# Moving the recurrent gate products of a pair of tiles behind both columns of the attention branch

## The reference, cut to what matters

```
xc = conv_b + sum_k conv_w[k] * shift(u_lru, k)                  # 4 taps
r = sigmoid(xb @ w_rg + b_rg);  i = sigmoid(xb @ w_ig + b_ig)    # 16 blocks of 64 features
log_a = -8 * r * softplus(-lru_lambda);  a = exp(log_a)
b = sqrt(-expm1(2 * log_a)) * (i * xc);  h_t = a_t * h_{t-1} + b_t
merged = g0 * (y_pool @ w_branch[0]) + g1 * (h @ w_branch[1]) + g2 * (y_sb @ w_branch[2])
```

## Time and profile before

| | |
|---|---|
| Median of 3 runs | 2202.89 us (2202.59 to 2204.14) |
| Profiled execution, its own time | 2201.45 us |
| Its span | 2199.6 us |
| Granted TensorE clock, mean | 0.997 |
| Busy: PE, PEld | 99%, 81% |
| Busy: DVE, ACT, POOL | 38%, 39%, 48% |
| Chain that ended last | PE 92%, DVE 4%, ACT 2% |

### The profile page before, as it was taken

How to read it: one execution, slowest core, us unless ns; L and a number is a source line. 1 busy time by engine, 2 the same in 40 slices (tenths; PEclk the granted TensorE clock), 3 DMA queues, 4 the chain that set the end, 5 groups by cost and what they waited for, 6 DMA issues and landing times.

```text
span 2199.6 us, 27553 instructions
## 1 busy us (share of the span) xinstructions
PE 2169.8 (99%) x10078; PEld 1788.5 (81%) x10078; DVE 844.8 (38%) x1310; ACT 855.8 (39%) x1209; POOL 1048.3 (48%) x882
## 2 busy tenths in 40 slices
PE   8999999999999999999999999999999999999998
PEld 6778777888888888888888888888887888888887
DVE  4244667632451111222376632322226555233212
ACT  4245686422242222222366533332224734333321
POOL 5431245655554444555455444445554535444553
PEclk9999999999999999999999999999999999999999
DMA  5221122322222222233221232223332212222222
GB/s 178 90 78 67 39 96 77 115 96 96 96 96 95 95 98 78 102 104 114 87 79 47 77 115 95 95 77 104 104 105 91 77 48 92 98 97 101 83 98 78
DMA packets 33848, 201.37 MB, mean 92 GB/s; under 512 B 3884, under 2 KB 6188, under 8 KB 15340
## 3 DMA queue, kind: packets, MB, share of 16 engines
q1 hardware_dynamic: 31532, 192.94, 25.6%
q0 software_dynamic: 2240, 7.40, 1.1%
HBM read 198.17 MB, written 2.15 MB: 91 GB/s over the span
## 4 chain that ended last, share of the span: by engine, by line
PE 92%; DVE 4%; ACT 2%; issue 1%; DMA 0%; DVEq 0%; SPq 0%; PEldq 0%; ACTq 0%
PE bank L416 28%; PE bank L417 28%; PE bank L418 28%; PE bank L659 2%; PE bank L957 1%; PE bank L646 1%; DVE pool_a L2350 1%; PE bank L917 1%; PE bank L971 1%; PE bank L633 1%; PE bank L632 1%; DVE temp_b L2166 0%; PE bank L627 0%; PE bank L629 0%; DVE temp_b L2355 0%
## 5 line engine op out<-in xcount | busy, mean ns | idle before, releaser
L1146 POOL TENSOR_TENSOR w_low<-raw,w_high 128x512 fp32r<-128x512 f32 (+2 forms) x768 | 961.9, 1283 | 1039.0 <-ACT w_high L1309 1000.6
L416 PE MATMUL bank<-x_low,w_high 128*128 128x512 f32 x1728 | 681.6, 394 | 13.1 <-DVE x_low L2162 9.5
L418 PE MATMUL bank<-x_high,w_low 128*128 128x512 f32 x1728 | 674.3, 390 | 0.0
L417 PE MATMUL bank<-x_high,w_high 128*128 128x512 f32 x1728 | 674.1, 390 | 0.0
L1309 ACT ACTIVATE w_high<-raw 128x2048 fp32r<-128x2048 f32 (+1 forms) x183 | 327.2, 1788 | 537.4 <-PE bank L418 537.4
L416 PEld LDWEIGHTS bank<-x_low,w_high 128*128 128x128 f32 x1728 | 325.1, 188 | 85.0 <-POOL w_low L1229 9.5
L417 PEld LDWEIGHTS bank<-x_high,w_high 128*128 128x128 f32 x1728 | 325.2, 188 | 68.3 <-issue 2.2
L418 PEld LDWEIGHTS bank<-x_high,w_low 128*128 128x128 f32 x1728 | 324.9, 188 | 67.7
L416 PE MATMUL bank<-act_low,w_high 128*128 128x512 f32 (+1 forms) x550 | 209.8, 381 | 0.0
L417 PE MATMUL bank<-act_high,w_high 128*128 128x512 f32 (+1 forms) x550 | 209.6, 381 | 0.0
L418 PE MATMUL bank<-act_high,w_low 128*128 128x512 f32 (+1 forms) x550 | 209.6, 381 | 0.0
(11 more groups left out here) (289 smaller groups left out, 2701.9 us busy)
## 6 DMA issues: line engine op xcount, KB each, us to landing
raw<-wmain SPq DMA_DIRECT2D x144, 1024.0 KB, 4.9
raw<-wdown SPq DMA_DIRECT2D x48, 704.0 KB, 4.0
bias<-distance_table POOLq DMA_DIRECT2D x24, 256.0 KB, 3.5
raw<-wmain SPq DMA_DIRECT2D x4, 512.0 KB, 8.6
x_residual<-x SPq DMA_DIRECT2D x4, 512.0 KB, 7.6
out<-qk SPq DMA_DIRECT2D x8, 256.0 KB, 2.2
matrices<-mats SPq DMA_DIRECT2D x1, 512.0 KB, 11.3
gate_blocks<-rg POOLq DMA_DIRECT2D x1, 512.0 KB, 6.4
```

What stands on the lines that cost most here:

```text
L416: pe.matmul(target, sh, ml, start=start and k == 0, stop=False)
L417: pe.matmul(target, sh, mh, start=False, stop=False)
L418: last = pe.matmul(target, sl, mh, start=False, stop=stop and k == n - 1)
L1146: pool.tensor_tensor(wl[:, c, part], raw[:, c, part], wh[:, c, part].bitcast(F32), ALU.subtract).then_inc(low_ready, 1)
```

## The change

In the loop over pairs, `sb_branch(t + 1)` is moved ahead of the two calls of `lru_gates`. PE then issues four columns in a row and the gate products behind them. Nothing else differs: the count of instructions, the semaphores that each waits for, the banks and the orders of the other engines are as they were.

```
                 lru(t + 1)
                 sb_branch(t)
+                sb_branch(t + 1)
                 lru_gates(t)
                 lru_gates(t + 1)
-                sb_branch(t + 1)
```

## The result

| | before | changed |
|---|---|---|
| Median | 2202.74 us (4 runs) | 2217.09 us (4 runs, 2216.87 to 2218.46) |
| Ratio of the runs | | 1.0069, 95% interval 1.0057 to 1.0081 |
| Profiled execution, its own time | 2201.45 us | 2218.46 us |
| Its span | 2199.6 us | 2216.7 us |

The change makes the kernel slower by 14.35 us (0.65%), against 14.6 forecast.

A forecast was written before the change was run, and what follows sets the result against it. PE, busy 99% of the span, was taken as the bound. Last pair's sigmoids 11.7 later + pooling chain 1.4 + half pace 1.5 = 14.6 us, 2217.5 on the median; own range 2213 to 2221, 8 in 10: 2207 to 2224.

The forecast's parts named there:

- S of the first pair: S is where ACT begins the sigmoids on a pair's gate products; in the first pair it comes 5.44 us later.
- interval of the gates: Pair loop on PE: late low pieces stall each pair about 2.3 us, so gate products begin 26.32 us apart.
- S of the last pair: Start of ACT's sigmoids in the last pair: 5.44 + 6.24 = 11.7 us later, from 348.40 to 360.1.
- chain from S to the third g0x column: Pooling stage, 68.30 us through ACT and DVE: POOL beside three DVE additions lengthens it 1.4 us, bounds 0 and 2.9.
- half pace behind the wait: PE's matmuls from the third g0x column: clock lowered after a 6.6 us wait, 1.5 us lost, bounds 0 and 1.5.
- The pooling chain hands on everything: Pooling stage: PE reaches the third g0x column 5.2 us early and waits, so the whole 11.7 us reaches the end time.
- A: Rival, pair loop: refill reaches PE without a stall, intervals 24.02 us, only the pooling chain hands on 4.8 us, 2207.7; chance 0.10.
- B: Rival: ACT and DVE catch up the 5.44 us before anyone needs them; not slower, 2200.4 us; chance 0.05.
- C: Rival, pair loop: DVE becomes the bound, slowed by POOL's low pieces, convolutions late, 6 us more, 2223.5; chance 0.12.
- D: Rival: nothing happens, since the gates were never near PE's path; 2202.9 us; chance 0.03.

The follow-up runs named there:

- run with the refill moved: Changed kernel with ACT's refill behind the g2y chunk moved ahead of the pair's recurrent sigmoids: 2207.35 us, ratio 1.0030.
- run with the first pair alone: Kernel before with sb_branch(t+1) moved ahead of the gates in the first pair only: 2208.45 us, ratio 1.0038.
- the early sigmoid: Sigmoids of the first two g0x columns moved on ACT ahead of the eighth pooling split: changed kernel 2209.11 us; kernel before 2198.43 us.
- run with POOL kept away: Changed kernel with mix_refill(16) moved on ACT from ahead of the eighth split to just behind it: 2216.65 us, ratio 1.0072.
- the filled wait: Changed kernel with 32 extra matmuls, results unused, in PE's queue in front of the third g0x column: 2214.90 us, ratio 1.0063.
- both runs of one pair: Kernel before with the new order in the first pair only, 2208.45 us, or in the last pair only, 2212.29 us.
- 24 extra matmuls: Changed kernel with 24 extra matmuls in PE's queue in front of the third g0x column: 2215.25 us.

## Why the prediction was right

The profiled executions, term by term:

| term | forecast | measured |
|---|---|---|
| S of the first pair | 5.44 | 281.02 - 275.69 = 5.33 |
| interval of the gates | 26.32 | 26.27 |
| S of the last pair | 11.7 | 11.42 |
| chain from S to the third g0x column | +1.4 | 71.68 - 68.30 = 3.38 |
| half pace behind the wait | 1.5 | 2.5 |
| sum | 14.6 | 17.3 (own times: 17.0) |

**S of the last pair** (11.7) is right in size and in each step: the refill at S + 9.51, POOL at S + 11.49, last piece, restart. The run with the refill moved shows that this is the way by which late gates reach PE: 2.37 us a pair vanish with it. The run with the first pair alone shows that the 5.2 us by which its first sigmoids came later are not caught up by anyone.

**The pooling chain hands on everything.** Right: with the early sigmoid the third g0x column starts 8.06 us sooner (423.44 against 431.50), and the changed kernel is 8.5 us over the kernel before on its chip where it was 14.35 on the first. PE came to the column 8.44 us early, where 6.6 was said, and where PE came itself was right to 0.2 us (431.50 - 8.44 = S + 63.2, forecast S + 63.1).

**The chain's growth** was mis-sized, 1.4 for 3.38. The mechanism is right: the run with POOL kept away gives the additions their 2.14 us back. The step that was off is "so I add half": it took a share of the 2.8 us in which POOL had been free, where each of the three additions had to be put at its price beside POOL, 1.68 for 0.72, 2.9 us in all. They lost 2.85 us (5.00 - 2.15). The small product behind them lost 0.94, and the subtraction behind that took 0.69 instead of 1.68, since POOL had finished by then. The last scan lost another 1.0 (2.19 against 1.22), which the prediction had priced for the convolutions but not for this chain; some 0.4 came back in the first two tiles. Of the range that I gave for it, 0 to 2.9, even the top would have been short.

**The half pace** was right as a mechanism, which the filled wait shows, and short by 1.0 in the profiled run: 13 steps from 431.50 to 437.08, 5.58 us, where 13 x 0.2265 + 0.12 = 3.06 would do. I took the start of the program as the price; there the slow steps were seven or eight, here twelve. The Trainium skill, "TensorE: Matmul & The Clock Gate", Part 1, has the array at half clock after an idle time until it has been busy for a while. The trace agrees in kind: the windows view of the changed kernel (busy time of PE, PEld, DVE, ACT, POOL, then granted clock, DMA share and GB/s) shows 0.50, that is 1.2 GHz, around the restart.

```profile
428.00:432.00 4.00, 0.50 (x1) 0.50 (x2) 1.44 (x3) 3.15 (x5) 0.03 (x1) 0.50 0.71 231
432.00:436.00 4.00, 4.00 (x11) 3.03 (x11) 1.82 (x3) 4.00 (x6) 0.94 (x1) 0.50 0.07 31
436.00:440.00 4.00, 4.00 (x17) 3.25 (x16) 1.00 (x2) 0.14 (x1) 4.00 (x4) 0.89 0.01 4
440.00:444.00 4.00, 4.00 (x20) 3.30 (x19) 0.00 (x0) 0.00 (x0) 0.08 (x1) 1.00 0.71 227
```

**The hit itself** (2217.5 for 2217.09) is better than the terms, and in part luck. The terms fall short of the profiled pair by 2.4 us; that pair lies 2.7 us further apart than the medians. The other three executions of the change have spans of 2215.1 to 2215.3, some 1.5 less than the profiled one, at a mean clock of 0.996 to 0.997 instead of 0.995. Whether they had fewer slow steps here or elsewhere, their traces would have to tell; on the later chip the change cost 15.7 us. With the two terms that were 3.0 us too small at their measured size the same sum would have said about 2220: the forecast hit because the medians lie closer together than the profiled pair.

**The rivals.** A fell: the intervals are not 24 us, unless the refill is moved. B fell with the result, and with both runs of one pair. C fell in the full change: the second scan does lose 1 us, the convolutions still end at 306.37 and the gates behind the stall do not wait. In the kernel with the first pair alone, where nothing covers them, they cost a wait of 3.34 us. D fell.

## What to carry to other kernels

Moving a short product later on the busiest engine delays not only its consumer but all that the consumer's engine has queued behind it. Here that was a refill of weights which did not need the product at all, and cost 2.37 us a pair. So read the queue of each waiting engine to its end and ask which entries PE needs next; if they don't depend on the late value, put them ahead of the wait, as the refill and the gate sigmoid here. The pooling chain, in which ACT and DVE only wait for each other, passed the delay on in full (68.30 and 68.38 us from S), however idle both look by their shares.

## What the runs showed that I had not expected

**Idle time costs again behind it.** 3.1 us of idleness were enough in the profiled run of the 24 extra matmuls for six slow steps, 4.9 us gave as many as 8.4 (twelve to fourteen, 2.5 us and more). The length of the wait does not settle it alone: in two other profiled runs 6.43 us gave eight slow steps and 7.26 gave twelve. Cutting the wait from 8.4 to 4.9 us by such filling gained nothing; cutting it to 1.3 gave back some 2.5 us of the profiled execution. Each count is of a single execution, so how sure the slow steps are at 3 us stays open.

**A dip of the clock far from the change.** In the profiled run of the kernel before, PE is at less than full clock in a stretch of the third block, with hardly any wait there:

```profile
1710.00:1720.00 10.00, 10.00 (x61) 8.71 (x59) 6.47 (x18) 6.29 (x17) 4.80 (x6) 0.87 0.50 158
```

In that of the early sigmoid the same stretch runs at full clock:

```profile
1708.00:1718.00 10.00, 10.00 (x69) 8.82 (x68) 7.06 (x20) 7.47 (x20) 5.09 (x7) 1.00 0.48 159
```

The dip is not the change's: over a window of 20 us the granted clock reads 0.91 there in ten of the thirteen profiled executions, the changed kernel's among them. It is missing in the three kernels with the early sigmoid. Set against the early sigmoid's execution, the same matmuls start 1.7 us later in that of before ahead of the stretch (at about 1709 us) and 3.2 us later behind it (at about 1740), so the dip costs some 1.5 us.

On the chip of these two kernels the executions of the kernel before range from 2198.79 to 2199.19 us where their mean granted clock is 0.999, up to 2204.0 where it is 0.997. So part of the 3.9 us between the medians is how many executions of either kernel lost clock. Among executions at 0.999 the gain is 1.7 us (fastest 2198.79 against 2197.10). With one profiled execution of each kernel, and with executions of before at 0.999 too (5 of 21 there, 7 of 15 on the chip where the refill was first moved), it isn't shown that the early sigmoid prevents the dip. What decides on it stays open.

**POOL and DVE slow each other by operation.** DVE's products, scans and additions with both inputs in SBUF lose about 1 us each beside POOL's subtraction (0.72 to 1.67, a third of 5.00, for an addition, 1.22 to 2.19 for a scan), a product of 16 columns too (0.17 to 1.12), while the convolution steps, with one input in PSUM, take 4.64 us for six at either time. POOL loses too: four of its subtractions take 5.01 us beside the convolutions and 6.00 beside DVE's pooling tiles. The Trainium skill, "GPSIMD Engine Reference", Specifications, names this contention for DVE instructions with two SBUF inputs; the trace agrees and gives it its size here.
